# Two-layer recurrence kernel: key gate inside the exponents, state steps in four parts, other rows between products and products between steps

## The reference, cut to what matters

```python
fp = heads(fg)
logf = jnp.logaddexp(jnp.log(lbh), jnp.log1p(-lbh) + jax.nn.log_sigmoid(fp))
kf = (1.0 - lbh) * jax.nn.sigmoid(-fp)
# scan over chunks, in each: cum = cumsum(logf)
attn = sum(q[t] * k[s] * exp(cum[t] - cum[s]))          # s <= t
o = attn @ v + (q * exp(cum)) @ state
state = exp(last) * state + (k * exp(last - cum)).T @ v
o = rmsnorm(o, g_hg_out) * silu(og)
u = cc * ch                                              # short convolution, width 3
conv = sum(ext[:, j:j + l] * w_conv[j] for j in range(3))
y_b = (cb * conv) @ w_br_b
```

## Time and profile before

| | |
|---|---|
| time, median of 3 runs | 1318.12 us (1316.23 to 1319.41) |
| the profiled execution | 1316.13 us, of which the span in the trace is 1314.4 us |
| TensorE matmul busy | 1179.3 us, 90% of the span |
| VectorE busy | 674.5 us, 51% |
| ScalarE busy | 251.8 us, 19% |
| GpSimd busy | 326.6 us, 25% |
| mean granted TensorE clock | 0.93 |

### The profile page before, as it was taken

One profiled execution on the slowest core, in us unless ns is written; L12 is line 12 of the kernel. 1 busy time (PEld: TensorE's weight loads), 2 busy tenths in 40 slices (PEclk: granted clock), 3 DMA queues, 4 the chain that ended last, 5 costly groups with the idle time before them and its releaser, 6 DMA issues. The chain is left out here.

```text
span 1314.4 us, 15369 instructions
## 1 busy us (share of the span) xinstructions
PE 1179.3 (90%) x5791; PEld 847.7 (64%) x5791; DVE 674.5 (51%) x1279; ACT 251.8 (19%) x470; POOL 326.6 (25%) x259
## 2 busy tenths in 40 slices
PE   4999989989999899788999999889699977888796
PEld 3888878768878777577888888444555534444342
DVE  6357886644478865544553535255433322222464
ACT  3232111002321100034211001011122221212222
POOL 2313433113144221133343443000222212121000
PEclk9999988889999788699999999989599998999999
DMA  6221211321211114341122242701689999999300
GB/s 207 65 66 63 65 33 51 100 82 65 93 59 42 33 51 121 127 121 65 65 70 91 90 145 67 296 32 37 253 332 376 378 383 392 387 392 336 141 33 36
DMA packets 99234, 191.82 MB, mean 146 GB/s; under 512 B 9126, under 2 KB 72438, under 8 KB 90968
## 3 DMA queue, kind: packets, MB, share of 16 engines
q1 hardware_dynamic: 93460, 181.73, 38.8%
q0 software_dynamic: 5440, 8.94, 2.1%
q10 hardware_dynamic: 260, 0.16, 0.0%
HBM read 180.68 MB, written 17.98 MB: 151 GB/s over the span
## 5 line engine op out<-in xcount | busy, mean ns | idle before, releaser
L1070 PE MATMUL ps<-arena,weights 128*128 128x272 f32 x2240 | 546.9, 406 | 9.1 <-ACT arena L688 8.2
L1070 PEld LDWEIGHTS ps<-arena,weights 128*128 128x128 f32 x2240 | 437.6, 197 | 111.6 <-issue 18.9
L562 POOL TENSOR_TENSOR weights<-weights 128x512 f32<-128x512 f32 x160 | 237.0, 1491 | 461.0 <-PE ps L1070 404.8
L1560 PE MATMUL ps<-arena 128*64 128x256 f32 x832 | 103.0, 404 | 24.6 <-DMA arena<-in_w_up 24.6
L1560 PEld LDWEIGHTS ps<-arena 128*64 128x64 f32 x832 | 60.8, 145 | 57.8 <-DMA arena<-in_w_up 26.5
L618 ACT ACTIVATE arena<-ps 128x272 f32<-128x272 f32 x80 | 31.6, 395 | 309.7 <-PE ps L1070 309.7
L1647 DVE TENSOR_SCALAR arena<-arena 64x256 f32<-64x256 f32 x32 | 9.1, 285 | 153.4 <-ACT arena L1611 153.4
L1105 PE MATMUL ps<-arena 128*128 128x64 f32 x448 | 69.3, 321 | 19.2 <-DVE arena L886 19.2
L1105 PEld LDWEIGHTS ps<-arena 128*128 128x128 f32 x448 | 66.1, 233 | 23.7 <-DVE arena L886 23.0
L1520 POOL DMA_INDIRECT expert_rows<-arena x32 | 29.3, 915 | 194.4 <-DVE arena L1662 194.4
L1239 PE MATMUL ps<-weights,arena 128*128 128x512 f32 (+1 forms) x160 | 69.1, 635 | 4.2 <-PEq L467 4.2
(11 more groups left out here) (240 smaller groups left out, 1307.8 us busy)
## 6 DMA issues: line engine op xcount, KB each, us to landing
weights<-in_w_in SPq DMA_DIRECT2D x36, 1024.0 KB, 5.1
arena<-in_w_gate SPq DMA_DIRECT2D x26, 1024.0 KB
arena<-in_w_up SPq DMA_DIRECT2D x26, 1024.0 KB
arena<-in_w_down SPq DMA_DIRECT2D x26, 1024.0 KB
weights<-in_w_gate SPq DMA_DIRECT2D x6, 1024.0 KB
weights<-in_w_up SPq DMA_DIRECT2D x6, 1024.0 KB
weights<-in_w_down SPq DMA_DIRECT2D x6, 1024.0 KB
arena<-in_x_prompt SPq DMA_DIRECT2D x8, 512.0 KB, 6.4
```

What stands on the lines that cost most here:

```text
L562: nc.gpsimd.tensor_tensor(SW[:, i], x, y, op).then_inc(s_ready, 1)
L1070: ins = mm(ps[:, b, 0:HF], w4[:, k, :], x4[:, k, :], start=(k == 0), stop=(k == 3))
L1560: ins = mm(ps[u * UP:u * UP + CAP, 2 + s, 0:DE], xgT[s][:, k, :], w[e % 5][:, k, :], start=(k == 0), stop=(k == KT - 1))
```

## The change: what it does

1. **Key gate in the exponents.** After the scans a new tile cK = cum - X is made, once for each group (X holds the log gate then). The key exponents of `kprep` and of each level are taken with cK in place of cum, so the multiplications by k (L866, L886) go. `gexp` on ScalarE now waits for cK.
2. **No clearing.** GpSimd no longer clears halves of Kl (L579), and VectorE no longer waits for it.
3. **Four steps.** `stB` is cut into `stB` (prompt output), `stC` (sample output) and `stD` (sample states). The wait for Vb is at `stD`. SyncE's stores stand at `stD`.
4. **Another weave.** `behind` is 6, 3, 4, 3, 4, 3, 4, 0, 1, then one product after each of twelve state steps, then 1, 0, 1, 0. The pairs of the convolution come in another order, and U has three buffers.
5. **Statistics in banks 4 to 7**, which the attention has left by then. The second of them waits until VectorE has copied the convolution's tail out of two of these banks.

```diff
-    def conv(p):
-        cb = pair("cb", p)
-        return pair("cc", p) + pair("ch", p) + cb[0:2] + [("conv", 2 * p)] + cb[2:4] + [("conv", 2 * p + 1)] + cb[4:]
+    def conv(g):
+        p, c = 2 * g, 4 * g
+        ch, cb = pair("ch", p + 1), pair("cb", p)
+        return (pair("cc", p) + pair("cc", p + 1) + pair("ch", p) + ch[0:6] + [("conv", c)] + ch[6:] + cb[0:1] + [("conv", c + 1)] +
+                cb[1:3] + [("conv", c + 2)] + cb[3:5] + [("conv", c + 3)] + cb[5:] + pair("cb", p + 1))
...
-            steps += [[("stA", h)], [("stB", h)]]
+            steps += [[("stA", h)], [("stB", h)], [("stC", h)], [("stD", h)]]
...
-    behind = [4] * LEV + [1, 1] + [2, 1] * GH
+    behind = [6, 3, 4, 3, 4, 3, 4, 0, 1] + [1] * 12 + [1, 0, 1, 0]
...
-        ev += weave(attention(g), conv(2 * g) + conv(2 * g + 1))
+        ev += weave(attention(g), conv(g))
...
+        elif kind == "stat":
+            for s in range(2):
+                use(("stat", x, s), 4 + (2 * x + s) % 4)
...
+        cK = area(R["oT@"] + 4 * T, GH * T).rearrange("p (h t) -> p h t", h=GH)
...
                 for kind, x in ev:
                     if kind == "pr" and PRODUCTS[x[2]] == "P7" and pair_no[x[0:2]] + 1 < len(pair_order):
                         weight_sums(pair_no[x[0:2]] + 1)
-                    if kind == "lev":
...
-                        nc.gpsimd.memset(v, 0.0).then_inc(kl_zeroed, 1)
...
-                        nc.scalar.activation(k, k, ACT.Exp).then_inc(a2d, 1)
+                        nc.scalar.activation(k, k, ACT.Exp).then_inc(lev_ready, 1)
...
+                        dve.wait_ge(dve_step, step.n)
+                        if x == 0:
+                            dve.wait_ge(tab_set, 16)
+                        v.tensor_tensor(cK, cum, X, ALU.subtract).then_inc(d2a, 1)
...
-                        for _ in range(4):
+                        for _ in range(3):
                             from_act()
-                        v.tensor_tensor(Kl, Kl, X, ALU.mult).then_inc(kt_ready, 1)
...
-                        c4, k4, x4, q4, Q4 = lvl(cum, l), lvl(Kl, l), lvl(X, l), lvq(l), lvl(Q, l)
+                        c4, k4, x4, q4, Q4 = lvl(cum, l), lvl(Kl, l), lvl(cK, l), lvq(l), lvl(Q, l)
...
                         v.tensor_tensor(q4, two(c4), mid, ALU.subtract).then_inc(d2a, 1)
-                        dve.wait_ge(kl_zeroed, LEV * g + l + 1)
-                        v.tensor_tensor(one(k4), mid, one(c4), ALU.subtract).then_inc(d2a, 1)
+                        v.tensor_tensor(one(k4), mid, one(x4), ALU.subtract).then_inc(d2a, 1)
                         from_act()
                         v.tensor_tensor(q4, q4, two(Q4), ALU.mult).then_inc(lev_ready, 1)
-                        from_act()
-                        v.tensor_tensor(one(k4), one(k4), one(x4), ALU.mult).then_inc(lev_ready, 1)
...
-                        pe.wait_ge(vb_ready, x + 1)
                         b = empty(("o", x))
...
+                    elif kind == "stC":
+                        g, h, s = x // 4, x % 4, x % 2
+                        hv = slice(h * P, h * P + P)
                         b = empty(("os", x))
                         pe.wait_ge(s0_loaded[s], 16 * (x // 2 + 1))
...
+                    elif kind == "stD":
+                        h = x % 4
+                        pe.wait_ge(vb_ready, x + 1)
...
                     elif kind == "stat":
                         from_dve()
+                        if x == 1:
+                            pe.wait_ge(tails_ready, 1)
```

More of the change, by code:

```diff
@@ L167, in layer @@
             first += 1
-        elif kind in ("xT", "stat"):
+        elif kind == "xT":
             for s in range(2):
@@ L230, in layer @@
               for at in (R["m@"], R["X@"] + 2 * KT * T, R["m@"])]
-        assert R["X@"] + 2 * KT * T + 16 * HF <= 17408 and 2 * HF + 2 * UW <= GH * UW
+        assert R["X@"] + 2 * KT * T + 16 * HF <= 17408 and 2 * HF + 3 * UW <= GH * UW
         W_flat = W[:, :, :, :].rearrange("p s k n -> p (s k n)")
@@ L567, in _ @@
                         weight_sums(pair_no[x[0:2]] + 1)
-                    if kind == "lev":
-                        g, l = x
-                        if l:
-                            full(pool, ("sc", (g, l - 1), 3))
-                        else:
-                            for h in range(GH):
-                                full(pool, ("kT", g, h))
-                            full(pool, ("kTs", g))
-                        v = lvl(Kl, l)
-                        v = v[:, :, 1, :] if len(v.shape) == 4 else v[:, :, :, 1, :]
-                        nc.gpsimd.memset(v, 0.0).then_inc(kl_zeroed, 1)
             @block.scalar
@@ L672, in _ @@
                         for j in (2 * x, 2 * x + 1):
-                            u = U[:, j % 2, :]
+                            u = U[:, j % 3, :]
                             from_dve()
@@ L816, in _ @@
                         link(v.scalar_tensor_tensor(R["qc"], R["X"], 0.0, R["Kl"], ALU.min, ALU.subtract))
-                        v.tensor_tensor(X, qc, X, ALU.subtract).then_inc(d2a, 1)
-                        last = None
+                        link(v.tensor_tensor(X, qc, X, ALU.subtract))
                         for h in range(GH):
@@ L852, in _ @@
                         from_act()
-                        dve.wait_ge(dve_step, step.n)
                         v.engine_nop().then_inc(d2a, 1)
@@ L934, in _ @@
                         v.engine_nop().then_inc(dve_state, 1)
-                    elif kind == "stB":
+                    elif kind == "stD":
                         h, s = x % 4, x % 2
@@ L948, in _ @@
                         for j in (2 * x, 2 * x + 1):
-                            u, y = U[:, j % 2, :], tmp[:, j % 2, :]
+                            u, y = U[:, j % 3, :], tmp[:, j % 2, :]
                             us = u[:, 2 + TP:UW].rearrange("p (b t) -> p b t", b=NB)
-                            if x == 0:
+                            if j < 3:
                                 link(v.memset(u[:, 0:2], 0.0))
@@ L957, in _ @@
                     elif kind == "conv":
-                        u = U[:, x % 2, :]
+                        u = U[:, x % 3, :]
                         us = u[:, 2 + TP:UW].rearrange("p (b t) -> p b t", b=NB)
@@ L1164, in _ @@
                             pe.wait_ge(p_loaded, 32)
-                            after_banks(pe, [("inc", 7), ("o", 7), ("os", 7), ("si", 7, 0), ("si", 7, 1)])
+                            after_banks(pe, [("stat", j, s) for j in (6, 7) for s in range(2)])
                         if x == 4:
```

15 lines of the change are left out of this document (8 added, 7 removed).

## The result

The changed kernel takes 1281.85 us (median of 4 runs, 1278.27 to 1289.72), the kernel before in the same comparison 1318.04 (1316.23 to 1319.41). The ratio is 0.9734 with a 95% interval of 0.9687 to 0.9781: faster, by 36 us where 54 to 56 were forecast, and 2 us above the range. The profiled execution took 1278.27 us, of which the span is 1276.6.

The account below looks back on a forecast made before the run. TensorE, busy for 90% of the span, was taken as the bound, losing time to waits and low clock in the attentions. Levels 43, states 3 and statistics 8 sum to 54 us off 1316.13, giving 1262 us; range 1242 to 1280.

Parts of the forecast that it names:

- Levels: Levels of both groups: all eight score-step waits (19.2 us) and the low clock (25.6) go, 2 kept back; gain 43 us.
- Masked copies beside sums: Levels: score copies reading PSUM are free beside GpSimd's sums; if they doubled, the levels' sum would fall by 2 to 4.
- States, the waits: States of both groups: a walk through one group gives waits of 10.4 us a group; the tail's 2.3 stays.
- States, the clock: States: three falls at 2.5 us a group remain; with the waits 38 us lost where 40.9 were, gain 3.
- the two low runs that touched now have a product between them, so the fall at the end of each head should mostly go: States, end of each head: a product between the two low-clock runs should mostly remove the fall; a remaining fall costs 2.5 us.
- a wait of 1.25 us as enough for a fall: States: such a wait had been enough for a clock fall, so new waits of 2.4 us or more may bring falls.
- My bound from below, a loss of 15: States: five waits of 2.6 and five falls of 2.8 us a group, 54 for both, lose 15 with the tail.
- The sign of being wrong that I had named, states over 85 us a group: Changed profile, states: a stretch over 85 us a group would show the forecast wrong.
- Statistics: Norm statistics: the next product no longer shares their banks, so the four waits for the logarithm go; gain 8.2 us.
- moves as it stands: Everything behind, from 640 us: it only shifts in time, with no gain or loss of its own.
- The front: Front of each group: exponential of X and `kprep` come 4.4 to 4.9 us later but are covered; cost nothing.
- the clock does not come back with the waits: Rival: levels return only 19.2 us, statistics 8.2, states nothing; 27 us gained, 1289 us; chance 0.07.

Follow-up runs that it names:

- e1: The kernel before with only the key gate in the exponents and no clearing; 1288.31 us, ratio 0.9806.
- e3: The changed kernel with the key multiplications and the clearing put back; 1287.05 us, ratio 0.9783.
- e7: The changed kernel with the convolution's pairs back in their old order; 1277.62 us, ratio 0.9717.
- e5: The changed kernel without the four-column matmuls of the sample output, so without its part from the old states; 1256.06 us, ratio 0.9547.
- e4: The changed kernel with prompt output, sample output and sample states in one step again and two products behind `stA`; 1265.59 us, ratio 0.9626.
- e9: The changed kernel with sample states loaded one head earlier and the convolution's arithmetic left out except one small instruction; 1256.16 us, ratio 0.9551.
- e10: As e9, also without the four-column matmuls of each head's sample output; 1233.49 us, ratio 0.9381.
- e2: The kernel before with only the statistics moved to banks 4 to 7; 1308.65 us, ratio 0.9972.
- r3_before: The kernel before, unchanged, profiled again; the two such repeat executions took 1313.21 and 1313.45 us.
- e13_later: The changed kernel with the four matmuls of one product behind the statistics done twice; 1279.53 us, ratio 0.9714.
- run 8: Not a follow-up run: the words tell of a run of four-column matmuls lying 8 us ahead of a wait in the changed kernel.

## Why the prediction was right or wrong

**Levels: right.** Forecast 43, by the table 44.5. One product a group moved from the levels into the states, though (458 matmuls for 467 before, 449 for 441 in the states; 1.85 us each), which my sum did not count on either side. Net of it the levels gave 40.8. All eight waits went, the clock came back with them, each group took 76.9 us. By e1 and e3 this has two causes that overlap: the shorter preparation, and the new places of products, sums and `conv`. The place of `conv`, with the order of its pairs, is worth 5.7 us a group (e7); what the place of the sums is worth alone was not measured.

**Masked copies beside sums: settled.** The copies at 146.00 and 146.69 lie inside the sums of 141.40 to 147.2 and took 0.42 and 0.45 us, as the two behind the sums did (0.44 and 0.43). The addition with two SBUF inputs at 142.20 took 1.04; the same addition took 0.44 at 782.68, where no sums run. The Trainium skill, "SBUF — State Buffer", section "Who interferes with whom", says that VectorE contends with GpSimd's reads where it has two SBUF inputs; this trace agrees.

**States, the waits: right.** Forecast 23.1 us with the tail's 2.3, measured 21.4. In group 0 the first three stand where the forecast put them: 2.13 at the diagonal (2.6), 1.69 ahead of the prompt output (1.5), 2.12 ahead of `stA` of head 1 (2.4). The next two came a head later: `stA` waited in head 3 (1.35), not in head 2 (1.0), and the load came late in head 3 (2.04), not in head 2 (2.7). The long fall in head 1 had given them time: in e5, which has no fall there, `stA` of head 2 waits 1.70 us, and the sample output of head 2 waits 2.44 for its load.

**States, the clock: the step that failed** is "the two low runs that touched now have a product between them, so the fall at the end of each head should mostly go". It does not go: e4, with no product between the two runs, lost as much (26.8 us) as the changed kernel (26.2). I put three falls at 2.5 us a group, 15 in all. The stretches lost 10.5 + 15.7 = 26.2, one fall alone 5.1. e9 and e10 show why: the four-column matmuls can bring the clock down without a wait near them, and in head 1 it then stays at 1.2 GHz through the sample states and another product. The same two stretches of before stood at 0.88 and 0.77 and lost 11.9 + 18.7 = 30.6: 4.4 less now, where the forecast had 14 come back (28.7 to 15). The forecast also took a wait of 1.25 us as enough for a fall. The earlier trace rows have it both ways: behind the wait at 133.50 four products ran at the full clock, behind the one near 156 the clock fell.

**States, the rest.** Waits 9.2 more (21.4 for 9.9 + 2.3), clock 4.4 less, the moved product 3.7: together 8.5 of the 11.1 us lost. The last 2.6 are what this sum leaves, and no run measured them alone. I had put them down to handovers between a product and a small step, which the cut made more of; but by the same sum e4, with two steps a head as before, leaves 1.2 (states 3.4 shorter, waits 4.5 less, clock 3.8 less, the product 3.7 more). So the cut accounts for about half at most, and the two digits of the clock blur it by 1 us. My bound from below, a loss of 15, held. The sign of being wrong that I had named, states over 85 us a group, came in group 1, at 87.0. e4 shows that the cut itself is the loss.

**Statistics: right, and then given back.** 8.2 forecast, 9.4 up to the output projection. The experts and the end took 5.7 back, where I had written that everything behind "moves as it stands". Of these, 3 us are the clock at the experts' start, which e2, with the move alone, has too. The end took 84.5 or 86.2 us in one kernel and the other alike (r3_before 86.1, e13_later 84.5), so I don't count that as an effect.

**The front: right.** Nothing was lost: the levels of group 0 start at 113.78 us, where they started at 113.85, and the rest of the front of group 1 took 61.1 us in both.

The sum: of the 16 us missing from 54, 11 are the clock in the states, 6 the experts and the end, 3 the unexplained rest of the states, 2 the levels, 22 in all; the waits (2), the statistics and routing (2) and a larger loss in the states before (2) give 6 back. Of the rivals, "the clock does not come back with the waits" fell in the levels and was half true in the states: e9 has 13.6 us of waits less than the changed kernel and 10 us less lost to the clock, but still 16. The fall at 228.99 came behind 10 us of work without a gap, and in e10, where eight short waits stayed and the small matmuls went, the clock held. The Trainium skill, "TensorE: Matmul & The Clock Gate", section "Why this matters for your kernels", says that longer idle gaps let the clock down. e10 is in line with that rule, and the fall at 228.99 is not explained by it.

## What to carry to other kernels

When a preparation is too long for its cover, look first at what stands beside and ahead of it: moving products, GpSimd's sums and `conv` (e3) freed the levels about as far as taking out a quarter of the preparation did (e1). Cutting a chain of small steps into more pieces, with other work between them, pays only if VectorE and the loads keep up; here it gave TensorE more places to wait, and a wait or a run of tiny matmuls costs its own time and often the clock's behind it. Before relying on a product to protect the clock, read in the trace how long the product behind such a run takes.

## What the runs showed that I had not expected

- A busy TensorE can lose its clock: sixteen 128x4 matmuls (1.95 us), no wait near, and then 11 us at 1.2 GHz (0.61 over 13 us). It happened behind five of eight such runs in the changed kernel and four of eight in e9. Without them, and with eight waits of at most 1.8 us left, the clock was 1.00 and 0.98.
- The same wait of 2.12 us brought a fall with such a run 8 us ahead of it (3.69 us for a product) and none without (2.00, in e5).
- The clock at the start of the experts differs with what was done 300 us earlier, in every profile: 8.5 us for 64 matmuls with the old banks, 11.5 with the new.
- The four sums on GpSimd took 5.80 us when they fell beside masked copies and additions, and 8.73 beside VectorE's long instructions with two SBUF inputs.
